# Projection units of two k tiles in the interleaved attention of a two-block kernel

## What is computed

```python
for l in range(2):
    hn = rmsnorm(h, norm_gain[l])
    dq, dk, dv, dg, fq, fk, fv, ff, fg = split(hn @ w_in[l])
    # four "diff" heads: q, k of two maps x 64, v of 128; partial rope on q and k
    a = softmax(q0 k0 * scale, chunk mask) - lam * softmax(q1 k1 * scale, chunk mask)
    do = rmsnorm(a @ v, subln_gain[l], 1e-5) * (1 - lam_init) * silu(dg)
    # eight "forgetting" heads of 64: s = q k * scale + c_q - c_k, c = cumsum(log_sigmoid(ff + bias))
    fo = softmax(s, causal mask) @ v * silu(fg)
    h = h + concat([do, fo]) @ w_out[l]
out = rmsnorm(h, final_gain)[:, 16:]
```

## Time and profile before

| | |
|---|---|
| runs | 2723.8 us median, 2722.2 to 2727.41 (3 runs) |
| execution profiled | 2731.44 us, its span 2729.6 us, granted clock 0.988 |
| PE busy | 2649.7 us, 97% |
| PE weight loads | 2278.5 us, 83% |
| DVE busy | 1637.5 us, 60% |
| ACT busy | 1201.0 us, 44% |
| POOL busy | 466.2 us, 17% |
| instructions | 43070 |

### The profile page before, as it was taken

One profiled execution on the slowest core, in us unless ns is written; L12 is line 12 of the kernel. 1 busy time (PEld: TensorE's weight loads), 2 busy tenths in 40 slices (PEclk: granted clock), 3 DMA queues, 4 the chain that ended last, 5 costly groups with the idle time before them and its releaser, 6 DMA issues.

```text
span 2729.6 us, 43070 instructions
## 1 busy us (share of the span) xinstructions
PE 2649.7 (97%) x16632; PEld 2278.5 (83%) x16632; DVE 1637.5 (60%) x2944; ACT 1201.0 (44%) x2372; POOL 466.2 (17%) x674
## 2 busy tenths in 40 slices
PE   6999999999999999999999999999998999999999
PEld 6888888888899888878777997888897788887887
DVE  5766664444535666554446366555437877778767
ACT  6444444333424444443334462223335655555444
POOL 2211232310001222452000124000013101011000
PEclk9999999999999999999999899999998999999999
DMA  4121377761312212897202423113232344444443
GB/s 150 57 67 64 120 191 198 202 158 44 142 58 74 74 64 74 245 233 182 82 24 78 129 72 114 47 47 100 93 92 95 116 127 121 124 126 153 177 154 135
DMA packets 219225, 314.21 MB, mean 115 GB/s; under 512 B 15478, under 2 KB 157494, under 8 KB 219022
## 3 DMA queue, kind: packets, MB, share of 16 engines
q0 software_dynamic: 50304, 151.30, 19.2%
q1 hardware_dynamic: 168720, 160.16, 18.6%
HBM read 267.26 MB, written 111.22 MB: 139 GB/s over the span
## 4 chain that ended last, share of the span: by engine, by line
PE 84%; DVE 6%; ACT 3%; issue 2%; DMA 2%; POOL 2%; SPq 0%; DVEq 0%; ACTq 0%; POOLq 0%
PE PS L1078 79%; PE PS L1087 5%; DMA T<-TMP 2%; DVE WL L2451 1%; DVE AL L2494 1%; POOL TMP L3427 1%; DVE ST L2623 0%; DMA R<-s_adap 0%; DVE TMP L2606 0%; POOL T L3424 0%; DVE T L2599 0%; ACT top L1881 0%; ACT TMP L1830 0%; DVE top L2636 0%; ACT TMP L1720 0%
## 5 line engine op out<-in xcount | busy, mean ns | idle before, releaser
L1078 PE MATMUL PS<-AH,WH 128*128 128x344 f32 (+2 forms) x2160 | 805.0, 373 | 23.7 <-DVE AL L2494 9.4
L1078 PE MATMUL PS<-AL,WH 128*128 128x344 f32 (+2 forms) x2160 | 756.8, 350 | 0.0
L1078 PE MATMUL PS<-AH,WL 128*128 128x344 f32 (+2 forms) x2160 | 756.3, 350 | 0.0
L1078 PEld LDWEIGHTS PS<-AH,WH 128*128 128x128 f32 x2160 | 408.8, 189 | 83.5 <-issue 21.0
L1078 PEld LDWEIGHTS PS<-AH,WL 128*128 128x128 f32 x2160 | 408.5, 189 | 36.0
L1078 PEld LDWEIGHTS PS<-AL,WH 128*128 128x128 f32 x2160 | 409.8, 190 | 32.1 <-issue 1.0
L1078 PE MATMUL PS<-WH,AH 128*128 128x256 f32 (+1 forms) x972 | 309.4, 318 | 3.7 <-DVE WL L2451 3.7
L1078 PE MATMUL PS<-WL,AH 128*128 128x256 f32 (+1 forms) x972 | 308.6, 317 | 0.0
L1078 PE MATMUL PS<-WH,AL 128*128 128x256 f32 (+1 forms) x972 | 308.6, 317 | 0.0
L2623 DVE TENSOR_REDUCE ST<-PS 128x1 f32<-128x784 f32 (+8 forms) x272 | 187.9, 732 | 143.0 <-PE PS L1078 142.5
L2451 DVE TENSOR_TENSOR WL<-W,WH 128x1024 fp32r<-128x1024 f32 x157 | 192.6, 1229 | 125.6 <-ACT WH L1708 125.5
(11 more groups left out here) (406 smaller groups left out, 4419.5 us busy)
## 6 DMA issues: line engine op xcount, KB each, us to landing
W<-in_k_w_in SPq DMA_DIRECT2D x66, 512.0 KB, 4.2
s_wt<-in_w_up POOLq DMA_DIRECT2D x96, 352.0 KB, 6.3
W<-in_w_ada SPq DMA_DIRECT2D x48, 512.0 KB, 5.2
s_wd<-in_w_down POOLq DMA_DIRECT2D x66, 256.0 KB, 6.3
W<-s_wt SPq DMA_DIRECT2D x64, 256.0 KB, 3.5
W<-in_w_in SPq DMA_DIRECT2D x28, 512.0 KB, 3.8
W<-in_w_up SPq DMA_DIRECT2D x52, 256.0 KB, 3.3
W<-in_w_out SPq DMA_DIRECT2D x24, 512.0 KB, 3.5
```

Source lines behind the costliest of these rows:

```text
L1078: return e.matmul(out, lhsT, rhs, start=start, stop=stop, skip_group_check=True)
```

## The change

A unit now covers two k tiles of its chunk, k and k + 1, six matmuls. `chunk` lists four units instead of eight, the planner's cost of one is doubled, and what was tied to the last k tile (7) is tied to the unit that starts at 6.

```diff
--- before.py
+++ after.py
@@ -481,7 +481,7 @@
             return steps
 
         def chunk(g, kind, ci):
-            steps = [("unit", g, kind, ci, k) for k in range(KT)]
+            steps = [("unit", g, kind, ci, k) for k in range(0, KT, 2)]
             if kind in "qk" and g < 4:
                 steps += [("late", n, (what, g, kind, ci)) for n, what in ((2, "rope"), (4, "rope_add"), (7 if g == 0 else 9, "rope_end"))]
             return steps
@@ -537,7 +537,7 @@
             def cost(self, st):
                 l, what = self.l, st[0]
                 if what == "unit":
-                    return 3 * (6.3 + 0.44 * cols_of(l, *st[1:3])[st[3]][1])
+                    return 6 * (6.3 + 0.44 * cols_of(l, *st[1:3])[st[3]][1])
                 if what == "scores":
                     g, j = st[1:]
                     cut = pieces(region(j, 0), region(j, 0) + width(j))
@@ -566,7 +566,7 @@
                         need.append(self.few[self.bank()][1])
                         if ci == 0:
                             need.append(at["lo", WI[l, g, kind]])
-                    if k == KT - 1 and (kind == "v" or kind in "qk" and g < 4):
+                    if k == KT - 2 and (kind == "v" or kind in "qk" and g < 4):
                         need.append(0.0 if self.tmp[ci] is not None else None)
                 elif what == "scores":
                     g, j = st[1:]
@@ -616,7 +616,7 @@
                     if k == 0:
                         self.take(key)
                         self.work = self.bank_of[key]
-                    if k == KT - 1:
+                    if k == KT - 2:
                         self.count += 1
                         self.few[self.work] = (self.count, None)
                         self.work = None
@@ -1003,7 +1003,7 @@
                     part = parts(l, g, bi)[n]
                     whole = part[-1] != BLOCKS[l][bi][-1] or part[0] == 8
                     PT_SIDE[l, g, bi, m, n] = EVICTS[l][g, bi, m, n] if whole else "both"
-                elif st[0] == "unit" and st[4] == 7:
+                elif st[0] == "unit" and st[4] == KT - 2:
                     _, g, kind, ci, _ = st
                     if kind == "v" or (kind in "qk" and g < 4):
                         TMP_FREED[l, g, kind, ci] = tmp[ci]
@@ -1160,9 +1160,10 @@
                         e.wait_ge(*cc.at(kk))
                     if ci == 0:
                         e.wait_ge(*w_lo.at(w))
-                wv = slice(128 * k, 128 * k + 128)
-                m = mm3(e, bank(at_work[0])[:, 0:n], WH[:, t, wv], WL[:, t, wv], AH[:, k, c:c + n], AL[:, k, c:c + n], k == 0, k == KT - 1)
-                if k == KT - 1:
+                for kk in (k, k + 1):
+                    wv = slice(128 * kk, 128 * kk + 128)
+                    m = mm3(e, bank(at_work[0])[:, 0:n], WH[:, t, wv], WL[:, t, wv], AH[:, kk, c:c + n], AL[:, kk, c:c + n], kk == 0, kk == KT - 1)
+                if k == KT - 2:
                     m.then_inc(*gemm_mm.mark(key))
                     banks.used(at_work[0])
                     at_work[0] = None
```

## The result

The changed kernel takes **2778.6 us** as a median of four runs (2777.04 to 2779.18) beside 2724.65 for the kernel before (2722.2 to 2727.41): a ratio of 1.0197, interval 1.0179 to 1.0214. It is 54 us slower, where 2728.5 was forecast with a range of 2715 to 2739.

The account below looks back on a forecast made before the run. PE, busy 97% of the span, was taken to bound the kernel. Terms of -1 + 3.3 + 2.4 - 3.3 - 2.8 + 4.6 + 1.5 summed to +4.7 us, a median of 2728.5 us, range 2715 to 2739.

Parts of the forecast that it names:

- Term 1: Whole kernel: fewer interruptions between runs of unit matmuls on PE, mostly given back by transposes; -1 us (-9 to 0).
- the rival of -9 by the change of step: Whole kernel, faster: the change of step is what costs, term 1 at -9 us, time 2716; chance 0.17 with other gains.
- Terms 2 and 3: Layer 0, heads 5 to 7: waits at tile 7's scores, +3.3 us; at chunk 2 of k, +2.4 us.
- The second slower rival: PE meets its banks too early in every head; terms 2, 3, 7 at upper ends, 13 us; 2733, chance 0.16.
- the rival of 2716: The faster rival: the change of step is what costs, term 1 at -9 us; chance 0.17 with other gains.
- Term 4: Layer 0, fin2 of heads 0 and 1: PE's idle waits for FIN go; -3.3 us (-3.3 to 0).
- Term 5: Tail of layer 1's attention: half clock goes as units spread later, with waits for copies and banks; -2.8 us (-5 to 0).
- Term 6: Behind layer 1's attention: POOL issues residual and R<-s_adap loads later, so tensor_mod waits; +4.6 us (0 to 9).
- Term 7: Layer 1, v of heads 5 to 7: turning v and transposes wait for banks, 0.5 us per head; +1.5 us.
- The prediction's own sign of being wrong: Layer 0, 94 to 720 us: PE idle below 8 or above 18 us would show the prediction wrong.
- The sign for term 6: Behind layer 1's attention: 4 to 6 us idle before the matmuls from COLS and R would show the prediction right.

Follow-up runs that it names:

- two tiles and both rules: The full change plus first unit of a chunk ranked first and POOL's weight sums issued behind a head's store, against the kernel before: 2725.01 us (1.0002).
- the wait of 16.4: PE's wait in layer 1 of the kernel before (one k tile) with first unit of a chunk ranked first; that run measured 2741.59 us (1.0056).

## Why the prediction was wrong

**Term 1, fewer interruptions: right for this change.** -1 was taken; span less idle less clock rose by 1.2 in layer 0 and 0.5 in layer 1. Counted from each matmul's start to the next one's (or to its own end before an idle gap) and less the half clock, unit matmuls took 13.8 us less over both layers and transposes 13.2 more, which is the give-back that the term argued with. With four tiles and 286 runs of units it is 28.7 less and 24.3 more. So the rival of -9 by the change of step fell, though there is a loose end: with two tiles and both rules (392 runs of units) the units took 13.4 less and the transposes only 3.2 more, and the remainder is 665.9 and 648.5 us, 8.6 less than before in sum. Its time equals that of the kernel before because these 8.6 stand against 6 us more idle time and 1 more of half clock. No run here tells why the give-back is missing there.

**Terms 2 and 3: right in place and size, and far too few.** In front of the scores of tile 7 PE waits 1.06 us in each of the heads 5, 6 and 7 (1.1 was taken, sum 3.2 for 3.3). In front of chunk 2 of k it waits 0.60 three times (0.8 was taken). But the prediction looked at the places where the distance between two known steps shrank. The same shortage of banks comes at almost every chunk: 0.66 at chunk 0 of k, 0.50 at chunk 1, 0.73 in turning v, 0.39 to 0.78 at the gate. This is the step that failed, the sum over places: 5.7 us stood for waits for evacuations that grew by 13.6 in layer 0. With what the sum had at nothing (4.8 for the exponential in layer 0, 14 behind the roots of both layers, 11 of half clock) that is most of the 48 us. That a rule for the first unit of a chunk and the place of a store took all of the loss away is what shows the cause.

**The second slower rival** (banks in every head, 2733, chance 0.16) named the mechanism. Its price was the upper end of the same three terms, 13 us, instead of waits counted over all chunk starts. By its own terms it should even have stood at 2737.6: its 9.1 us more were added to the 2723.8 of before and not to the forecast of 2728.5 (the rival of 2716 has the same slip). Its argument against, that ACT and DVE are far from full, carried nothing: an engine at 40% is late in each single case if two copies and a chunk's end come together.

**Term 4: half right.** No FIN matmul waits any more, but in the same places transposes wait 1.85 us each and a short av 0.65 and 0.70: nothing came back. What was late next had not been asked; for the first of the transposes it is a DVE step on the probabilities (L2640) that ends 0.1 us before them.

**Term 5: right.** The piece of 6.8 us at half clock is gone; the last stretch of layer 1 after the change is

```profile
1540.00:1547.70 7.70, 6.21 (x45) 4.21 (x41) 3.83 (x8) 3.24 (x5) 0.00 (x0) 1.00 0.01 2
```

with one wait of 1.49 us in it where 1.6 and 0.7 were taken.

**Term 6: right chain, no cost.** POOL and tensor_mod behind layer 1:

```profile
1551.71 4.17 POOL L3455 DMA_DIRECT2D top<-s_hs  x8
...
1558.95 4.40 POOL L3484 DMA_DIRECT2D R<-s_adap  x8
```

The residual's loads come 4.0 us after the out projection begins (3.5 to 4.5 was said), and R is waited for 1.8 us instead of 0.58. From the out projection's start to tensor_mod it is 26.0 us against 23.5. Yet from there to the end all is made up, in a place that was not looked for: the part behind layer 1 takes 1229.7 us, before 1230.0. 4.6 was taken, with 0 as the bound.

**Term 7: wrong place.** At turning v of these heads PE waits twice 0.25 us, where 1.5 was taken. The waits of layer 1 are two of over 4 us behind a root, and small ones at chunk starts between 1045 and 1199 us (1.07, 0.70 and 1.05).

**Not in the prediction at all:** that ACT's root blocks evacuations for 4.7 us, 14 us in three places; and that PE runs at half clock behind waits of a few us, which cost 11 us more than before in sum. The range had no room for either, since the waits of terms 2, 3 and 7 were priced by their own length. The prediction's own sign of being wrong, PE idle above 18 us in layer 0 from 94 us on, came: it was 10.4 and is 33.3. The sign for term 6, 4 to 6 us idle in front of COLS and R, did not.

One number of its working has no row: the traces record 16,632 matmuls on PE in both kernels, where it says 15,576. It is not in the sum.

Two rules stood beside the terms. By the Trainium skill (TensorE: Matmul & The Clock Gate, "Step-by-step: what each phase is for") weight loads are pulled ahead of matmuls in flight, and by that alone a change of step would be free. In sum the trace agrees in the comparison of the two kernels, +1.2 and +0.5 us with 91 fewer runs of units; with two tiles and both rules it does not, -8.6 us with 108 fewer. By the Trainium skill (DMA: Bandwidth & Descriptors, "Anatomy of one DMA — SWDGE (gpsimd) path") a DMA has a fixed cost of about 2.0 us, and by that R would have landed in time (as an estimate from that page, some 10 us before PE wanted it in the kernel before, not the 8 of term 6); the trace does not agree, R was waited for 1.8 us and landed 10.9 us after its last issue.

## What to carry to other kernels

Where several kinds of work share a few buffers, look at who takes the last free one: a coarser unit makes other work ready in pairs, and a pair that ranks first takes the buffer that the bottleneck's next block needs. Reserving it by rank repaired 37 of 54 us here and, with one store put ahead of the weights in its queue, all of it: units of two tiles then cost nothing in sum. If the kernel holds a planner with clocks, read the waits that it books for both orders and test them against the trace before, where they can be seen to agree; and count waits over every place of the kind, not over the places where the change is seen first. An order planned with a fixed price for a store is blind to what stands ahead of it in a DMA queue.

## What the runs showed of the hardware

- Half clock stood behind waits of 1.85 us already (191.0 to 194.5 us), once behind small ones alone, of 0.67 and 0.50 (587.0 to 590.4), and about 17 us of it around the wait of 16.4. How much there is varies with the same order: 15.8 us lost to the clock in layer 0 of the change, 11.1 in the run on layer 0 alone.
- Seven of the fourteen stores of a head's output in the kernel before land 3.0 us after their issue or sooner. The one at 1141.1 takes 9.4 although no further weights are put ahead of it: the last transfers of the sum before, issued until 1135.8, land until 1148.2, the store at 1150.5. With 14 more transfers ahead of it on the same queue it is issued at 1154.1, lands at 1167.1 and holds PE up for 14.5 us.
